# Two sets of PSUM banks for the gate and up rounds of a mixture, and scores issued earlier in four attentions

## What is computed

```
first_block:   h += even_mixer(...)                 # short convolution and pooling
               h += cross_attn(h, mem)              # 4 heads of 256, 256 memory tokens
               h += swiglu(...)
               h += conformer_conv(...)
               h += cross_attn(h, mem)
               h += moe_swiglu(...)                 # 8 experts, 2 per token, inner width 3584
second_block:  h += even_mixer_2(...)               # block attention and differential attention
               h += grouped mixture                 # 16 experts, 2 per token, inner width 256
               h += odd_mixer_2(...)                # compressed, selected and window attention
               h += grouped mixture

def moe_swiglu(xn, router, w_gu, w_down):
    w = softmax(top_k(xn @ router, 2))
    for e in range(8):
        out += comb[..., e] * ((silu(xn @ w_g[e]) * (xn @ w_u[e])) @ w_down[e])

def cross_attn(xn, mem, ...):
    p = softmax(q @ k.T * XATTN_HEAD_DIM ** -0.5)
    return (p @ v) @ wo

def diff_attention(q, k, v, lam):                   # q and k rotated, causal
    w = p[:, :, 0] - lam * p[:, :, 1]               # two softmax maps a head
    return w @ v

def nsa_attention(q, kc, vc, ks, vs, kw, vw, gates):
    p_c = softmax(q @ kc.T)                         # over 15 compressed blocks
    o = gt[0] * (p_c @ vc) + gt[1] * o_selected + gt[2] * o_window
```

## Time and profile before

| | us |
|---|---|
| median of 3 runs | 2494.61 |
| lowest, highest | 2491.35, 2498.98 |
| profiled execution | 2497.58 |
| its span | 2495.8 |
| mean granted TensorE clock | 0.970 |
| TensorE busy | 2363.4 |
| VectorE busy | 687.6 |
| ScalarE busy | 376.7 |
| first mixture | about 800 to 1693 |
| block and differential attention, maps | 1808 to 1848 |
| compressed attention, maps | 2199 to 2262 |

### The profile page before, as it was taken

One profiled execution on the slowest core, in us unless ns is written; L12 is line 12 of the kernel. 1 busy time (PEld: TensorE's weight loads), 2 busy tenths in 40 slices (PEclk: granted clock), 3 DMA queues, 4 the chain that ended last, 5 costly groups with the idle time before them and its releaser, 6 DMA issues.

```text
span 2495.8 us, 34659 instructions
## 1 busy us (share of the span) xinstructions
PE 2363.4 (95%) x14928; PEld 1358.6 (54%) x14928; DVE 687.6 (28%) x1507; ACT 376.7 (15%) x812; POOL 1.2 (0%) x9
## 2 busy tenths in 40 slices
PE   8899999999999999999999999998979998989997
PEld 6777888878676333333333333336665336756433
DVE  2575122149665101011010101101242122263122
ACT  1101100010121110101110111111032111153212
POOL 0000000000000000000000000000000000000000
PEclk9899999999999999999999999998989998989999
DMA  9488154564274998999999999997403996532591
GB/s 328 159 298 329 68 197 174 175 218 164 102 261 180 340 357 334 357 407 409 404 409 405 407 406 391 363 404 270 142 27 106 343 342 133 160 104 73 198 347 47
DMA packets 281384, 645.13 MB, mean 258 GB/s; under 512 B 14699, under 2 KB 99969, under 8 KB 281217
## 3 DMA queue, kind: packets, MB, share of 16 engines
q1 hardware_dynamic: 278444, 637.64, 69.6%
q10 hardware_dynamic: 2773, 5.11, 0.6%
HBM read 641.66 MB, written 1.05 MB: 258 GB/s over the span
## 4 chain that ended last, share of the span: by engine, by line
PE 86%; DVE 7%; issue 2%; ACT 2%; SPq 1%; DMA 1%; ACTq 0%; DVEq 0%
PE bank L1549 20%; PE bank L1267 19%; PE bank L1651 11%; PE bank L1586 7%; PE bank L1491 6%; PE bank L1503 3%; PE bank L1287 3%; DVE att L3264 2%; PE bank L1578 2%; PE bank L1711 2%; PE bank L1670 1%; PE bank L1316 1%; SPq L1177 1%; PE bank L1637 1%; PE bank L1797 1%
## 5 line engine op out<-in xcount | busy, mean ns | idle before, releaser
L1549 PE MATMUL bank<-ring,xn 128*32 128x512 f32 (+1 forms) x3520 | 470.2, 597 | 18.4 <-DVE sq L2871 15.2
L1267 PE MATMUL bank<-xn,ring 128*128 128x256 f32 x2048 | 452.9, 383 | 2.6 <-issue 1.0
L1267 PEld LDWEIGHTS bank<-xn,ring 128*128 128x128 f32 x2048 | 391.9, 192 | 60.7 <-issue 7.4
L1549 PEld LDWEIGHTS bank<-ring,xn 128*32 128x32 f32 (+1 forms) x3520 | 142.7, 115 | 322.1 <-issue 315.8
L1651 PE MATMUL bank<-ring,att 128*32 128x512 f32 x2208 | 247.9, 593 | 1.3 <-ACT att L2328 1.3
L2871 DVE TENSOR_TENSOR sq<-att,bank 32x512 f32<-32x512 f32 x70 | 48.0, 686 | 432.7 <-ACT att L2339 431.1
L1651 PEld LDWEIGHTS bank<-ring,att 128*32 128x32 f32 x2208 | 72.1, 110 | 160.3 <-issue 159.9
L1491 PE MATMUL bank<-xn,ring 128*128 128x256 f32 x704 | 152.8, 379 | 0.0
L1491 PEld LDWEIGHTS bank<-xn,ring 128*128 128x128 f32 x704 | 133.8, 190 | 18.3
L2339 ACT ACTIVATE att<-bank 64x512 f32<-64x512 f32 (+1 forms) x123 | 72.4, 589 | 375.7 <-PE bank L1549 290.9
L2328 ACT COPY att<-bank 128x384 f32<-128x384 f32 (+1 forms) x72 | 29.9, 450 | 539.0 <-PE bank L1637 419.3
(11 more groups left out here) (345 smaller groups left out, 1936.2 us busy)
## 6 DMA issues: line engine op xcount, KB each, us to landing
ring<-od_moe_gu SPq DMA_DIRECT2D x196, 1024.0 KB, 12.8
ring<-od_moe_down SPq DMA_DIRECT2D x49, 2048.0 KB, 16.5
ring<-ada_w SPq DMA_DIRECT2D x24, 2048.0 KB, 8.6
ring<-moe_w_gate SPq DMA_DIRECT2D x32, 1024.0 KB, 11.0
ring<-moe_w_up SPq DMA_DIRECT2D x32, 1024.0 KB, 10.2
ring<-moe_w_down SPq DMA_DIRECT2D x16, 2048.0 KB, 13.7
z<-od_moe_gu SPq DMA_DIRECT2D x28, 1024.0 KB, 11.5
ring<-ev_w_in SPq DMA_DIRECT2D x10, 2048.0 KB, 20.0
```

Of the source, the lines that this page charges most:

```text
L1267: mm = nc.tensor.matmul(ps[:, c * T:(c + 1) * T], kblk(b)[:, k, u * T + c * P:u * T + (c + 1) * P], x[:, k, :], start=k == 0, stop=k == KD ...
L1549: mm = nc.tensor.matmul(PSB[r.fill.b][j * w:(j + 1) * w, :], xn[:, k, at:at + w], rows_[:, half, c * WBLK:(c + 1) * WBLK], start=k == 0, s ...
```

## The change

**First mixture.** Rounds of a double alternate between banks (0, 1, 2) and (3, 6, 7). A chunk's turn goes into a bank of its own double's rounds; the last turn and `place` go into bank 7; the previous expert's results go into banks 4 and 5, those of the down products. The order of instructions stays the same on every engine. Here is TensorE's queue where an expert's second double begins (bank numbers shown, with the waits of an instruction). Before:

The core of the diff:

```diff
--- before.py
+++ after.py
+                banks = ROUND_BANKS[d % 2]
...
                 if paired:
-                    x.rounds = [tiles_round(fill(b), 2) for b in range(x.n)]
+                    x.rounds = [tiles_round(fill(b), 2) for b in banks[:x.n]]
...
-                    x.rounds = [tiles_round(fill(0), 4), tiles_round(fill(1), 2 * x.n)]
+                    x.rounds = [tiles_round(fill(banks[0]), 4), tiles_round(fill(banks[1]), 2 * x.n)]
...
-                        x.three = tiles_round(fill(2), 4)
+                        x.three = tiles_round(fill(banks[2]), 4)
...
                 if d:
-                    for c in st.doubles[-1].c:
-                        c.turn = fill(TURN_AT[c.c % 2])
+                    for c, b in zip(st.doubles[-1].c, ROUND_BANKS[(d - 1) % 2]):
+                        c.turn = fill(b)
                         down_block(st, c, down, tiles)
+                    if d == 2:
+                        st.place = fill(ROUND_BANKS[1][2], placed)
...
-            c.turn = fill(TURN_AT[c.c % 2])
+            c.turn = fill(ROUND_BANKS[1][2])
             down_block(st, c, down, tiles)
...
-        TURN_AT = 7, 3
+        ROUND_BANKS, RESULT_BANKS = ((0, 1, 2), (3, 6, 7)), (4, 5)
...
-                j.s_fill, j.t_fill = fill((0, 1, 6)[i % 3]), fill(2 + i % 2, (probT_ready, count(probT_ready, 1) + 1))
+                j.s_fill, j.t_fill = fill((6, 7, 1)[i % 3]), fill(2 + i % 2, (probT_ready, count(probT_ready, 1) + 1))
...
+        SCORE_PAIRS = (6, 7, 4), (0, 1, 4)
...
+                freed = (score_ready, st.score + 3 * u.i + 3)
+                u.early_fill = fill(at[2], freed) if len(at) > 2 else fill_turn(freed)
...
+            def score_banks(u):
+                return pairs[u.i % 2] if pairs else [SCORE_BANKS[(3 * u.i + k) % 5] for k in range(3)]
...
-            return [fill(TURN_AT[i % 2], (h_ready, count(h_ready, 1) + 1)) for i in range(4)]
+            return [fill(RESULT_BANKS[i % 2], (h_ready, count(h_ready, 1) + 1)) for i in range(4)]
...
-        ev2.att = maps(units, (att, kT.rearrange("p k t -> p (k t)")))
+        ev2.ropes = [rope_linear(W2, at * MW, MW) for at in (0, 1, 3)]
+        ev2.lam_fill = fill_turn()
+        ev2.ropes.append(rope_linear(W2, 4 * MW, MW))
+        ev2.att = maps(units, (att, kT.rearrange("p k t -> p (k t)")), begun=True)
+        ev2.va = token_linear(W2, 2 * MW, MW, proj_ready)
+        ev2.att.score_fills(units[0], (6, 7))
+        ev2.att.score_fills(units[1], (6, 7))
+        ev2.vb = token_linear(W2, 5 * MW, MW, proj_ready)
+        ev2.att.rest()
+        for i, u in enumerate(units):
+            u.rotated = (rope_ready, ev2.ropes[1 if i < 2 else 3].rope + i % 2 + 1)
+            u.projected = (proj_ready, (ev2.va if i < 2 else ev2.vb).end)
...
+            u.rotated, u.projected = (rope_ready, od2.q.rope + i // 2 + 1), None
...
-        od2.cturn = fill(TURN_BANKS[1], (csoft_ready, od2.csoft + 4))
-        od2.att = maps(units, (att, z[:, 8:14, :].rearrange("p k t -> p (k t)")))
+        od2.att = maps(units, (att, z[:, 8:14, :].rearrange("p k t -> p (k t)")), begun=True, pairs=SCORE_PAIRS)
+        od2.att.score_fills(units[0], SCORE_PAIRS[0])
...
+        od2.by_block = fill(5, (blockwise_ready, 1))
+        od2.att.score_fills(units[1], SCORE_PAIRS[1])
+        od2.cscore = fill(5, (csoft_ready, od2.csoft + 1))
+        od2.att.rest(lambda: fill(TURN_BANKS[1], (csoft_ready, od2.csoft + 4)))
...
-                for j in js[:3]:
-                    scores(j)
+                for i in range(len(js)):
+                    q_unit(i)
+                    if i:
+                        scores(js[i - 1])
+                scores(js[-1])
                 for i, j in enumerate(js):
-                    if i + 3 < len(js):
-                        scores(js[i + 3])
                     turned(j)
...
             pe_linear(r[0], xn, normed(twin))
             pe_linear(r[1], xn, None)
             rotate(r[0], 0)
-            pe_token_linear(ev2.va, xn)
+            pe_linear(r[2], xn, None)
             rotate(r[1], 4)
-            pe_linear(r[2], xn, None)
-            pe_linear(r[3], xn, None)
-            rotate(r[2], 8)
-            pe_token_linear(ev2.vb, xn)
-            rotate(r[3], 12)
             pe.wait_ge(lam_ready, 1)
             ps = open_bank(ev2.lam_fill)
             nc.tensor.matmul(ps[:, 0:2], ones[0:1, :], lam[0:1, 6:8], start=True, stop=True)\
                 .then_inc(bank_full[ev2.lam_fill.b], 1)
-            pe.wait_ge(rope_ready, r[3].rope + 2)
-            pe.wait_ge(proj_ready, ev2.vb.end)
-            pe_maps(ev2.att)
+            pe_linear(r[3], xn, None)
+            rotate(r[2], 8)
+            scores, rest = pe_maps(ev2.att)
+            for i, (b, c, f) in enumerate(ev2.va.units):
+                if i == 0:
+                    landed(b)
+                else:
+                    scores(ev2.att.units[0])
+                token_unit(b, c, f, xn)
+            rotate(r[3], 12)
+            scores(ev2.att.units[1])
+            pe_token_linear(ev2.vb, xn)
+            rest()
...
+            scores, rest = pe_maps(od2.att)
+            pe.wait_ge(dup_ready, od2.kv[1].dup + 2)
+            scores(od2.att.units[0])
...
+            ps = open_bank(od2.by_block)
+            for half in range(2):
+                for q in range(4):
+                    i = 4 * half + q
+                    g = i // 2
+                    mm = nc.tensor.matmul(ps[q * QP:(q + 1) * QP, half * T:(half + 1) * T],
+                                          kcmp[:, g // 2, g % 2].rearrange("p h n -> p (h n)"), z[:, i, :],
+                                          start=True, stop=True)
+            mm.then_inc(bank_full[od2.by_block.b], 1)
+            scores(od2.att.units[1])
+            pe.wait_ge(blockwise_ready, 1)
             ps = open_bank(od2.cscore)
             for c in range(TC):
-                for i in range(NSA_H // 2):
-                    g = i // 2
-                    at = c * T + i * 2 * NCMP_PAD
-                    mm = nc.tensor.matmul(ps[:, at:at + 2 * NCMP_PAD], z[:, i, c * P:(c + 1) * P],
-                                          kcmp[:, g // 2, g % 2].rearrange("p h n -> p (h n)"), start=True, stop=True)
+                for half in range(2):
+                    mm = nc.tensor.transpose(ps[:, c * T + half * P:c * T + (half + 1) * P],
+                                             raw_cmp[:, half, c * P:(c + 1) * P], ident)
             mm.then_inc(bank_full[od2.cscore.b], 1)
-            pe.wait_ge(dup_ready, od2.kv[1].dup + 2)
 
...
                 js = st.jobs
+                beside(0)
+                beside(1)
                 scores(js[0])
+                beside(2)
                 scores(js[1])
-                for i, j in enumerate(js):
-                    if i + 2 < len(js):
-                        scores(js[i + 2])
-                    probs(j)
-
-            def dve_maps(st, second=None):
+                probs(js[0])
+                beside(3)
+                scores(js[2])
+                probs(js[1])
+                scores(js[3])
+                probs(js[2])
+                probs(js[3])
...
+            ev2_tmp = att[:, 8 * T:10 * T].rearrange("p (c t) -> p c t", c=2)
+            rotary(ev2.ropes[0], 0, ev2_tmp)
+            rotary(ev2.ropes[1], 4, ev2_tmp)
             f = ev2.lam_fill
             nc.vector.tensor_copy(lam[:, 0:2], full(f)[:, 0:2]).then_inc(bank_free[f.b], 1)
             freed(f)
-            dve_maps(ev2.att)
+            rotary(ev2.ropes[2], 8, ev2_tmp)
+            scores, probs, rest = dve_maps(ev2.att)
+            scores(ev2.att.units[0])
+            probs(ev2.att.units[0])
+            rotary(ev2.ropes[3], 12, ev2_tmp)
+            scores(ev2.att.units[1])
+            probs(ev2.att.units[1])
+            rest(2)
...
+            scores, probs, rest = dve_maps(od2.att)
+            scores(od2.att.units[0])
...
+            scores(od2.att.units[1])
+            normalise_compressed()
+            rest(1)
             add_chunks([f for b, u, f in od2.out.units], lambda k: mod[:, 1, 2, k:k + 1], ALU.mult, then=moe2[1].norm)
             dve_experts(moe2[1])
```

204 lines of the change are left out of this document (114 added, 90 removed).

## The result

The changed kernel takes 2454.04 us, the median of 4 runs (2450.82 to 2463.15), where the kernel before took 2494.61 us, the median of 3 runs (2491.35 to 2498.98). A fourth run of the kernel before took 4132.37 us, far from all others here, and is left out. The ratio is 0.9842, with a 95% interval of 0.9804 to 0.988: between 30 and 49 us less. The forecast was 2466, the range 2451 to 2481: the result lies 12 us under the forecast and 3 us above the lower end of the range. The profiled execution took 2455.47 us with a span of 2453.7, 42.1 less than the span before.

What follows compares the result with a forecast made beforehand. TensorE's work, holes and slow clock were taken as the bound. Gains of 16.4 + 9.3 + 1.0 + 1.0 + 0.6 = 28.3 us gave 2466 us against the 2494.6 median, range 2451 to 2481.

Steps and rivals of the forecast that it cites:

- The mixture's sum: First mixture: bank waits removed plus clock regained, less what late data takes back; 16.4 us gained.
- the 6.0 given back: First mixture: removed waits of the third, fourth and fifth expert only lengthen the wait for data; 6.0 us not gained.
- the last three: First mixture: bank waits after 1347 us, 2.8 + 2.8 + 1.6 us, kept as gain because TensorE waits for no data there.
- Rival A: First mixture data bound to its end: 9.2 us in place of 16.4, whole 2473 us; chance 0.15.
- The new wait: First mixture: first down matmul needs the previous expert's results added from banks 4 and 5; this wait should be empty.
- Diff attention: Diff attention: early scores laid among value projections and last rotation, so unit 2's scores start sooner; 9.3 us gained.
- Cross attentions: Both cross attentions: a head's scores follow the next head's query projection, shortening softmax waits; 1.0 us gained in each.
- Compressed attention: Compressed attention: wide products, with scores of unit 0 before them; 0.6 us gained, ends −4 and +4.
- X: Compressed attention: time when the compressed scores end, taken as 2201.6, the mean of full and half clock.
- Rival B: Attentions give nothing, since VectorE's steps are one chain and waits only move; whole 2475 us; chance 0.14.
- rival C: Compressed attention: shared bank 4 makes TensorE wait in each unit and the clock fall; slower, 2504 us; chance 0.04.
- Rival D: Whole kernel: every wait named goes, 44 us gained, 2451 us; chance 0.07.

Runs made afterwards that it cites:

- the kernel with D of 18.3: Changed kernel with compressed attention reordered on three engines, units 0 and 1 scored before compressed keys; folding to unit 3's scores 18.3 us; 2448.39 us.
- the first of the two versions: Changed kernel with unit 1's scores before the compressed products, and VectorE making them before the mask; 2457.39 us, ratio 0.9836.

## Why the prediction was right, and where it was off

- **The mixture's sum** (16.4) was right, and so were its parts: the two waits before 1060 us with their clock (10.0 forecast, 9.6 measured), the 6.0 given back (measured: all of it), the last three (7.2 forecast, 6.5). The 0.8 taken off for a fall of the clock near 1347 has no counterpart: the clock was 1.00 from 1060 to 1500. That the sum agrees to 0.3 is partly luck, as the stage scatters by 2.4 us. Rival A, 9.2 in all, is out. The new wait, for results in banks 4 and 5, was empty as said. What the prediction quoted from the Trainium skill ("TensorE: Matmul & The Clock Gate", section "HAM oscillation — how this bites in real kernels") on double buffering, no further gain, does not carry over to this loop: 16.1 us, not 0.
- **Diff attention** (9.3): 10.0. The step "scores of unit 2 start 9.3 sooner" measured 1822.38 − 1791.40 − 21.38 = 9.6, with 21.38 the lead at the norm before. As forecast, the wait of 1.69 us of unit 3's scores for exps is still there (1797.39).
- **Cross attentions** (1.0 and 1.0): 2.6 and 1.5. In the first, I kept a third of the waits where nearly all go. Both are within the ends of +3.
- **Compressed attention** (0.6): 10.9, outside the ends of −4 and +4. The step that failed is X, the end of the compressed scores, which I set at 2201.6. Measured from the folding, X was forecast at 2201.6 − 2185.1 = 16.5 us and is 2161.75 − 2150.77 = 11.0. I started from 2192.0, a time that half clock and small waits had already made late, and put 2.3 us of scores on top; yet with unit 0's scores in front, the products start 6.7 us after the folding, where they had started after 7.0 without them. The scores cost nothing (2.3 forecast), as they lie in ScalarE's time, and the clock was 1.00 to the transposes where I took the mean of both clocks (3.2 more); that is the 5.5. The chain behind X was right in length: 12.3 + 2.9 = 15.2 forecast, 14.7 measured (2176.48 − 2161.75). Its place was not: unit 2's early scores want bank 4 as well, after unit 1's, so TensorE waits one unit earlier than I said. D is shorter by 3.0 from X and by 3.6 from what lies behind it (14.7, where it was 18.3).
- **3.2 us of the 10.9 lie ahead of the folding,** where the order is the same in all kernels. The folding comes 97.3 us after the norm in the mean of the four kernels with the old order (96.5 to 97.8) and 94.2, the mean of four, with the new one. The difference is in holes in the middle of the hidden products, which nothing in the profile releases: 3.7, 3.8, 3.7 and 2.6 us there, and 2.2, 2.1, 0 and 0 here. But the kernel with D of 18.3 has 3.8 as well (1.40 and 2.41), the first of the two versions 3.5, and the one with narrow products 0. So neither order alone sets them, what sets them stays open, and these 3.2 us can't be counted for the change. The other 7.7 lie behind the folding: 6.7 in the two profiled executions of before and after; the other three kernels with the old order have some 3 us more of half clock there and take 1.4 to 1.5 us longer.
- **Rival B** is out by the stage's 10.0, **rival C** too: one hole came and not one in each unit, the clock was half for 10.2 us behind it, from 2174 on it was 1.00, and a unit took 6.66 us as before. The prediction's condition for it, the size of the hole, was read too simply: 2.81 us at 1170 left the clock alone, but 2.81 at 958 did not. VectorE's unit is 10 instructions and 5.6 us, for the 11 and 5.4 of the prediction; it stays below 6.7 all the same.
- **Rival D** (every wait goes, 44 us, 2451) is the nearest in the total, by another way: its mixture (20), diff attention (14) and cross attentions (6) are too large by 3.9, 4.0 and 1.9, and its compressed attention (4) is too small by 6.9. The range held since it was set wide enough for that; 12 us of the gain were not foreseen, and 10 of them are the one term whose ends the result left.
